# The first block's gates as a strand of their own, two heads' scores in one bank, norm factors applied behind the products, and a first mixer that does not yield to the second tile's block

## The chip, the cores and the metric

One core of a Trainium2 chip runs the whole program. The metric is the device time of one launch, in microseconds. The kernel before took 2147.11 us (median of three runs, 2147.04 to 2147.55).

## The reference

256 tokens of width 1024 pass one block of the first kind and two layers of the second kind, all in f32. Cut to what matters here:

```python
# first block (DEPTH = 1)
proj = rmsnorm(x, mix_norm_g) @ w_in            # 2560 columns of q/k/v, 3072 of gates
mkv  = rmsnorm(mem, mem_norm_g) @ w_mem_kv
gates = sigmoid(graw).reshape(B, S, 3, D_MODEL)
o_a = moba_attention(rope(rmsnorm(qa)), rope(rmsnorm(ka)), va) @ w_branch_moba     # 6 heads
o_d = dilated_attention(rope(rmsnorm(qd)), rope(rmsnorm(kd)), vd) @ w_branch_dil   # 6 heads
o_m = memory_attention(rmsnorm(qm), rmsnorm(mk), mv) @ w_branch_mem                # 4 heads
x = x + (gates[:,:,0]*o_a + gates[:,:,1]*o_d + gates[:,:,2]*o_m) @ w_out
u = causal_depthwise_conv(rmsnorm(x, ffn_norm_g) @ w_ffn_up)                       # 5632 columns
x = x + (silu(u_gate) * u_val) @ w_ffn_down
# second block, twice (l = 0, 1)
proj = rms_norm(x, norm1_g[l]) @ w_in[l]        # attention, convolution, RG-LRU
x = x + concat(forgetting_attention, conformer_conv, rglru_block) @ w_out[l]
xn = rms_norm(x, norm2_g[l])                    # peer: 8 heads route each token to 16 experts
x = x + sum_k gate_k * gelu(xn . u_tab[e_k]) * v_tab[e_k]      # 128 experts for each token
```

The expert tables are `peer`, one row of 8 KB (a row of u beside a row of v) for each expert. A token needs 128 rows in a layer.

## The kernel before

**Tiles and stages.** The tokens are two tiles, t = 0 and 1, of 128 on the partitions. B0 and B1 are the first block for the tiles, M00, M01, M10, M11 the mixers for layer l and tile t (M00 is layer 0, tile 0). A mixer ends with the routing, four times two heads, each of which writes 32 columns of `eidx` (L1802). Then come 128 gathers for this layer and tile: gather k brings the rows of expert k of all 128 tokens, 1 MB, by an indirect DMA of GpSimd (L2082). For each gathered MB VectorE makes a dot product with xn (`dot`, L1931), ScalarE a weight (`weigh`), and either TensorE adds the scaled row into PSUM (`down`, L1070) or VectorE adds it into x (L1941). There are 512 gathers, and none of a tile can start before its routing.

**Weights.** They are streamed as slabs of 2 MB (1.5 or 1 MB for some) into `ring`, three places of 16 KB a partition, by SyncE's queue (`slab`, L2098), in the order in which TensorE takes them (`take`); a slab is loaded once the slab three places before it (two, from the first gather on) is used up. A block takes 5 slabs of q/k/v, for B0 one of the memory, 6 of gates, 3 branches, 2 of w_out, 11 up and 6 down; a mixer takes 11. A token tile (L723) is 8 matmuls of 512 columns for each slab, a feature tile (L737) 32 of 128 columns. The trace has two records for each such f32 matmul, so a slab is 16 or 64 records.

**Places for gathered rows.** There are eight of 1 MB: 0 to 3 are `arena`, free when M00's key scores are done (`key_scores`); 4 and 5 are `kv1`, which holds the keys and values of the first block until the attention of B1 is over (`att_over`); 6 and 7 are the third place of `ring`.

**Order.** Each engine has a strand for each stage, written as a generator that yields after each step. A planner inside the program (`make_plan`) runs the strands against costs written by hand and writes a fixed order for TensorE, VectorE and ScalarE. Among the steps that are ready it takes the least `wish`, which is 1 plus 0.01 for each place in `STAGES`, so an earlier stage first. One rule speaks of M00: while TensorE has made fewer than `T_HEAD` = 80 steps of B1, M00 (with its strands R00 and C00) has the wish 1.3 and comes after B1. Engines run their fixed order; one that waits holds up all that stands behind it.

**B0.** Its gates run in `gate_chunks`, woven step by step with the heads by `weave` on all three engines. The norm of a tile is a chain (`rms_tile`): ScalarE squares, VectorE inverts, ScalarE takes the root, VectorE refines (`newton`) and multiplies x into scr (`scaled`, L1578); TensorE transposes that, then multiplies. The memory has the same chain (`mem_scaled`, L1590).

**Attention** goes by units of two heads: `scores` (L768), the row maximum on VectorE (L1469, or L1473 without a mask), the exponential on ScalarE, for the dilated heads counts on VectorE (L1484), transposes (L784), a copy, and `values` (L798). The scores of a unit have two PSUM banks, one for each head. Room.S, T and O are the banks for scores, transposes and outputs: B0 has two pairs for scores and one bank each for T and O; M00 and B1 have one of each.

## Time and profile before

| | |
|---|---|
| median of 3 runs | 2147.11 us |
| the profiled execution | 2146.26 us |
| its span | 2144.5 us |
| PE, DVE, ACT, POOL busy | 81%, 63%, 38%, 28% |
| DMA moved | 774.29 MB, mean 361 GB/s |
| granted clock of TensorE, mean | 0.92 |
| first gather | 534.5 us |

The page divides the span into 40 slices of 53.6 us. Its line DMA gives the mean busy share of the 16 DMA engines in tenths, and is read beside the line of PE: at each place one of the two is near 9. A timeline row gives the start and the length of a run of like instructions, the line of the kernel, and in brackets the idle time of that engine before it with what ended it.

### The profile page before, as it was taken

The page shows a single profiled execution, that of the slowest core. Times are in us where ns is not written, and L with a number is a line of the kernel's source. Part 1 is how long each engine was busy: PE and PEld are TensorE (multiplying, and loading weights), DVE is VectorE, ACT ScalarE, POOL GpSimd, SP SyncE. Part 2 cuts the span into 40 slices and gives each one's busy share as a digit, 9 for nine tenths or more (in the row PEclk, how much of TensorE's full clock was granted, in tenths as well). Part 3 has the DMA queues.
Part 4 walks back from the last instruction along what each step waited for, and adds up shares of the span by engine and source line. Part 5 has one row for each costly group of instructions (what it writes and reads, how often), then busy time and mean ns, then how long its engine had stood idle before and what let it go on. Part 6 is the DMA issues. An engine that isn't in the chain of part 4 may idle for free.

```text
span 2144.5 us, 21045 instructions
## 1 busy us (share of the span) xinstructions
PE 1746.1 (81%) x6904; PEld 1012.3 (47%) x6904; DVE 1348.5 (63%) x3432; ACT 807.3 (38%) x2104; POOL 595.3 (28%) x516
## 2 busy tenths in 40 slices
PE   7988989889878888977767877767798777677776
PEld 3447847547567464453324633623364362222222
DVE  2423314713988558757886786588888658885444
ACT  2232201520456436523434354134437414333333
POOL 0000000000222223533444353234443324434331
PEclk9989999799989999989989898978999988879999
DMA  9556767157999999999999999999999998999997
GB/s 359 214 199 235 290 241 293 50 229 263 385 417 406 418 414 407 416 420 406 410 409 418 411 412 402 419 361 419 420 419 420 419 378 321 394 383 415 420 420 311
DMA packets 108526, 774.29 MB, mean 361 GB/s; under 512 B 12160, under 2 KB 12416, under 8 KB 16256
## 3 DMA queue, kind: packets, MB, share of 16 engines
q0 software_dynamic: 73728, 536.90, 61.2%
q1 hardware_dynamic: 34688, 236.04, 27.8%
q8 instruction: 54, 0.88, 0.2%
q14 instruction: 56, 0.46, 0.1%
HBM read 771.85 MB, written 1.05 MB: 360 GB/s over the span
## 4 chain that ended last, share of the span: by engine, by line
PE 40%; DMA 34%; DVE 14%; issue 5%; ACT 4%; POOL 3%; SPq 0%; DVEq 0%; POOLq 0%; ACTq 0%
DMA kv<-in_peer_dram,eidx 12%; PE psum L1070 10%; DMA arena<-in_peer_dram,eidx 10%; PE psum L723 8%; PE psum L737 8%; DMA ring<-in_slabs_dram 7%; PE psum L927 5%; DMA ring<-in_peer_dram,eidx 4%; PE psum L945 3%; POOL arena L2082 1%; DVE arena L1931 1%; PE psum L902 1%; DVE kv L1931 1%; DVE x L1941 1%; DMA wf<-in_wf_dram 1%
## 5 line engine op out<-in xcount | busy, mean ns | idle before, releaser
L1070 PE MATMUL psum<-arena,diag 128*128 128x512 f32 x824 | 425.5, 651 | 127.9 <-ACT diag L1393 124.8
L2082 POOL DMA_INDIRECT arena<-in_peer_dram,eidx x258 | 306.3, 1187 | 479.3 <-PE psum L1070 367.6
L1931 DVE CUSTOM_DVE_ANT_0 arena<-arena,osb 128x1024 f32<-128x1024 f32 x258 | 314.0, 1223 | 163.4 <-DMA arena<-in_peer_dram,eidx 162.7
L2082 POOL DMA_INDIRECT kv<-in_peer_dram,eidx x130 | 147.8, 1137 | 828.5 <-DVE eidx L1802 534.0
L1383 ACT ACTIVATE wexp<-hid 128x1 f32<-128x1 f32 x512 | 103.0, 201 | 702.4 <-DVE hid L1931 701.6
L1070 PEld LDWEIGHTS psum<-arena,diag 128*128 128x128 f32 x824 | 159.2, 206 | 355.0 <-ACT diag L1393 198.8
L1070 PE MATMUL psum<-kv,diag 128*128 128x512 f32 x428 | 219.0, 640 | 60.7 <-ACT diag L1393 56.7
L723 PE MATMUL psum<-ring,hT 128*128 128x512 f32 x560 | 252.0, 603 | 4.4 <-DMA ring<-in_slabs_dram 1.6
L1070 PE MATMUL psum<-ring,diag 128*128 128x512 f32 x376 | 197.0, 654 | 71.5 <-ACT diag L1393 71.3
L1931 DVE CUSTOM_DVE_ANT_0 kv<-kv,osb 128x1024 f32<-128x1024 f32 x130 | 158.6, 1222 | 82.4 <-DMA kv<-in_peer_dram,eidx 81.9
L737 PEld LDWEIGHTS psum<-hT,ring 128*128 128x128 f32 x1536 | 184.3, 199 | 34.6 <-DMA ring<-in_slabs_dram 18.1
L2082 POOL DMA_INDIRECT ring<-in_peer_dram,eidx x124 | 141.0, 1137 | 213.2 <-PE psum L1070 176.4
L737 PE MATMUL psum<-hT,ring 128*128 128x128 f32 x1536 | 185.4, 283 | 17.4 <-DMA ring<-in_slabs_dram 15.2
L1931 DVE CUSTOM_DVE_ANT_0 ring<-ring,osb 128x1024 f32<-128x1024 f32 x124 | 151.0, 1223 | 59.1 <-DMA ring<-in_peer_dram,eidx 58.6
L927 PE MATMUL psum<-hT,ring 128*128 128x130 f32 x1408 | 169.2, 283 | 18.4 <-DMA ring<-in_slabs_dram 9.2
L927 PEld LDWEIGHTS psum<-hT,ring 128*128 128x128 f32 x1408 | 167.9, 198 | 28.3 <-issue 15.6
L723 PEld LDWEIGHTS psum<-ring,hT 128*128 128x128 f32 x560 | 106.8, 194 | 133.0 <-issue 126.9
L1393 ACT ACTIVATE diag<-const,wexp 128x128 f32<-128x128 f32 x407 | 163.4, 401 | 13.4
L1070 PEld LDWEIGHTS psum<-kv,diag 128*128 128x128 f32 x428 | 81.9, 203 | 171.8 <-ACT diag L1393 89.8
L1070 PEld LDWEIGHTS psum<-ring,diag 128*128 128x128 f32 x376 | 73.8, 207 | 178.1 <-ACT diag L1393 105.1
L1386 ACT ACTIVATE wexp<-wexp,sm 128x1 f32<-128x1 f32 x512 | 150.8, 294 | 16.6
L945 PE MATMUL psum<-ring,scr 128*128 128x512 f32 x176 | 80.1, 614 | 11.7 <-DMA ring<-in_slabs_dram 11.7
(315 smaller groups left out, 1794.1 us busy)
## 6 DMA issues: line engine op xcount, KB each, us to landing
ring<-in_slabs_dram SPq DMA_DIRECT2D x206, 1024.0 KB, 6.9
ring<-in_slabs_dram SPq DMA_DIRECT2D x8, 768.0 KB, 5.5
arena<-in_peer_dram,eidx POOLq DMA_INDIRECT x258
ring<-in_slabs_dram SPq DMA_DIRECT2D x8, 512.0 KB, 4.3
kv<-in_peer_dram,eidx POOLq DMA_INDIRECT x130
kk<-in_keys_dram SPq DMA_DIRECT2D x2, 1024.0 KB, 11.0
ring<-in_peer_dram,eidx POOLq DMA_INDIRECT x124
rowg<-in_rows_dram SPq DMA_DIRECT2D x3, 512.0 KB
```

Of the source, the lines that this page charges most:

```text
L723: ins = pe.matmul(bank(b), hT_[:, k, :], wk[:, k, :], start=(k == 0), stop=(k == 7))
L737: ins = pe.matmul(bank(b)[:, 128 * i:128 * i + 128], wk[:, k, 128 * i:128 * i + 128], hT_[:, k, :], start=(k == 0), stop=(k == 7))
L902: ins = pe.matmul(bank(b), oT[:, k0 + k, :], wk[:, k, 512 * h:512 * h + 512], start=(k == 0), stop=(k == kb - 1))
L927: ins = pe.matmul(bank(b)[:, 256 * gv:256 * gv + 130], wk[:, k, cw:cw + 128], hTe[:, k, :], start=(k == 0), stop=(k == 7))
L945: ins = pe.matmul(bank(b), act[:, f, :], wk[:, k, 512 * h:512 * h + 512], start=(f == 0), stop=(f == 21))
L1070: ins = pe.matmul(bank(b), diags_of(n), pair(slot_of[n])[:, 1024 + 512 * h:1536 + 512 * h], start=(k == 0), stop=(k == 127))
L1383: act.activation(wn, hid[:, 128 * t + k:128 * t + k + 1], ACT.Gelu_apprx_tanh).then_inc(*up("gelu", n))
L1386: act.activation(wn, wn, ACT.Copy, scale=gate[t][:, k:k + 1]).then_inc(*up("weight", n))
L1393: act.activation(diags_of(n), ident, ACT.Copy, scale=wn).then_inc(*up("diag", n))
L1931: v.tensor_tensor_reduce(out=row, in0=row, in1=row_y[t], scale=1.0, scalar=0.0, op0=ALU.mult, op1=ALU.add, accum_out=hid[:, c:c + 1]).then ...
L1941: v.scalar_tensor_tensor(x3[:, t, :], pair(slot_of.get(n, 0))[:, 1024:2048], wexp[:, c:c + 1], x3[:, t, :], ALU.mult, ALU.add).then_inc(*u ...
L2082: pool.indirect_dma_start(pair(i), None, tables, bass.IndirectOffsetOnAxis(ap=eidx[:, 128 * t + k:128 * t + k + 1], axis=0)).then_inc(sig. ...
```

## The change

1. **T_HEAD is 0**, so M00 never has the wish 1.3 and stands before B1 at every choice.
2. **Gates as a strand.** B0's six gate slabs become a stage G0 of their own, with a place in `STAGES` right behind B0; its loads stand in the order in which it takes them. The first branch of B0 waits for the last gate.
3. **Two heads' scores in one bank.** `scores` writes both heads into one bank, and the second head's matmul waits until the first has ended (`pe_step`). The banks that come free give B0 a second one for T and for O, M00 and B1 a second one for scores, and the later mixers a second one for T.
4. **Norms behind the products.** For the first norm of B0 and B1 and for the memory, the raw x is transposed and multiplied, and the factor is applied as `scale` of the ScalarE copy or sigmoid that empties the bank. The two kinds of scaling on VectorE (`scaled` "h", `mem_scaled`) are gone; the norm before the FFN and those of the mixers stay.

```diff
-T_MB, T_SEEN, T_ISSUE, T_DOT, T_WEIGHT, T_DIAG, T_TENSOR, T_VECTOR, T_TABLE, T_HOP, T_KEEP, T_LEAN, T_AHEAD, T_LATE, T_PACE, T_SHRINK, T_FLIGHT, T_END, T_HEAD = 2.5, 2.0, 1.15, 1.35, 0.55, 0.42, 2.0, 1.35, 1.28, 0.12, 4, -2.0, 14, 0.0, 3.0, 0, 8, 0, 80
+T_MB, T_SEEN, T_ISSUE, T_DOT, T_WEIGHT, T_DIAG, T_TENSOR, T_VECTOR, T_TABLE, T_HOP, T_KEEP, T_LEAN, T_AHEAD, T_LATE, T_PACE, T_SHRINK, T_FLIGHT, T_END, T_HEAD = 2.5, 2.0, 1.15, 1.35, 0.55, 0.42, 2.0, 1.35, 1.28, 0.12, 4, -2.0, 14, 0.0, 3.0, 0, 8, 0, 0
...
-            "B0": Room(range(8), (0, 6), (2,), (4,), scr, hT, tmp),
-            "M00": Room((0, 1, 2, 3, 0, 1, 2, 3), (0,), (2,), (3,), arena[:, 0:2816], arena[:, 3072:5120], arena[:, 5120:8192]),
-            "B1": Room((4, 5, 6, 7, 4, 5, 6, 7), (4,), (6,), (7,), scr, hT, tmp),
+            "B0": Room(range(8), (0, 1), (2, 6), (4, 7), scr, hT, tmp),
+            "M00": Room((0, 1, 2, 3, 0, 1, 2, 3), (0, 1), (2,), (3,), arena[:, 0:2816], arena[:, 3072:5120], arena[:, 5120:8192]),
+            "B1": Room((4, 5, 6, 7, 4, 5, 6, 7), (4, 5), (6,), (7,), scr, hT, tmp),
         }
         for m in ("M01", "M10", "M11"):
-            room[m] = Room((4, 5, 1, 3, 4, 5, 6, 7), (4, 6), (1,), (3,), scr, hT, tmp)
+            room[m] = Room((4, 5, 1, 3, 4, 5, 6, 7), (4, 6), (1, 5), (3,), scr, hT, tmp)
...
-        STAGES = ("B0", "M00", "R00", "C00", "B1", "Q00", "M01", "R01", "C01", "Q01", "M10", "R10", "C10", "Q10",
+        STAGES = ("B0", "G0", "M00", "R00", "C00", "B1", "Q00", "M01", "R01", "C01", "Q01", "M10", "R10", "C10", "Q10",
...
@@ -760,16 +764,19 @@
 
                 def scores(i):
                     u, n = units[i], r.S[i % len(r.S)]
-                    s3 = psum[:, 512 * n:512 * n + 1024].rearrange("p (h k) -> p h k", h=2)[:, :, 0:u.nk]
+                    s3 = bank(n).rearrange("p (h k) -> p h k", h=2)[:, :, 0:u.nk]
                     for done in ready:
                         w.wait_ge(*done)
+                    wait_bank(n)
                     for h in range(2):
-                        wait_bank(n + h)
                         ins = pe.matmul(s3[:, h, :], u.q(h), u.k(h), start=True, stop=u.bias is None)
                         if u.bias is not None:
                             ins = pe.matmul(s3[:, h, :], *u.bias(h), start=False, stop=True)
+                        if h == 0:
+                            ins.then_inc(*own.up())
+                            w.wait_ge(*own.now())
                     ins.then_inc(*up("att_scores", s, i))
-                    bank_free[n] = bank_free[n + 1] = at("att_top", s, i, 1) if u.mask is not None else at("att_exp", s, i, 1)
+                    bank_free[n] = at("att_top", s, i, 1) if u.mask is not None else at("att_exp", s, i, 1)
...
-                yield from turn_tile(s, scr_[:, 0:1024], b_[6:8], "turned_v", at("scaled", s, "h"), "h")
+                yield from turn_tile(s, x3[:, t, :], b_[6:8], "turned_v", (sig.sem("l_x%d" % t), 16), "h")
...
-                if t == 0:
-                    yield from weave(heads(), gate_chunks())
-                else:
-                    yield from heads()
+                yield from heads()
...
+                    if t == 0:
+                        w.wait_ge(*at("gates_out", t, 5))
...
+            def first_gates():
+
+                b_, hTt = room["B0"].bank, hT_tile("B0")
+                w.wait_ge(*at("turned_v", "B0", "h", 1))
+                for c in range(6):
+                    after = at("gates_out", 0, c - 2) if c > 1 else at("mem_out", 1, 1) if c else at("turned_v", "B0", "h", 1)
+                    yield from token_tile("G0", (b_[5], b_[3])[c % 2], hTt, "gates", 0, c, after=after)
...
                     w.wait_ge(*at("qkv", t, c))
+                    w.wait_ge(*at("rms", s))
                     for i, (d, of) in enumerate(pieces(s, t, c)):
-                        act.activation(d, bank(b_[c % 2])[:, of], ACT.Copy).then_inc(*up("qkv_out", t, c, i))
+                        act.activation(d, bank(b_[c % 2])[:, of], ACT.Copy, scale=sm[:, 641 + 3 * t:642 + 3 * t]).then_inc(*up("qkv_out", t, c, i))
...
-                y = yield from rms_tile(s, "h")
-                w.wait_ge(*own.now())
-                v.tensor_scalar(xs, x3[:, t, :], y, None, ALU.mult).then_inc(*up("scaled", s, "h"))
+                yield from rms_tile(s, "h", "rms", s)
...
-                        for u in range(2):
-                            v.tensor_scalar(mem_s[:, u, :], mem3[:, u, :], ym[:, u:u + 1], None, ALU.mult).then_inc(*up("mem_scaled", u))
```

**TensorE around M00's key scores, before.** `kk` are the keys; L737 with `arena` is M00's query projection, L723 with `hT` a gate or w_out slab of B1, L902 a branch of B1:

```order
L723 MATMUL psum<-ring,arena 128x512 x16
L723 MATMUL psum<-ring,hT 128x512 x6
L751 MATMUL psum<-const,osb 128x128 x8
L737 MATMUL psum<-arena,ring 128x128 x128
L902 MATMUL psum<-ring,scr 128x512 x3
L1036 MATMUL psum<-kk,arena 128x128 x16
L902 MATMUL psum<-ring,scr 128x512 x3
L723 MATMUL psum<-ring,hT 128x512 x16
```

**After**, the same place (line numbers are 4 to 8 higher: L741 is the old L737, L1044 the old L1036, L873 the old L872, the transposes of B1's queries and keys; L772, L791, L805 the attention):

```order
L755 MATMUL psum<-const,osb 128x128 x8
L727 MATMUL psum<-ring,hT 128x512 x6
L741 MATMUL psum<-arena,ring 128x128 x64
L727 MATMUL psum<-ring,hT 128x512 x2
L741 MATMUL psum<-arena,ring 128x128 x64
L873 MATMUL psum<-const,scr 128x128 x4
L1044 MATMUL psum<-kk,arena 128x128 x16
L873 MATMUL psum<-const,scr 128x128 x10
L772 MATMUL psum<-kv,scr 128x256 x4
```

Before, B1's whole attention, four of its gate slabs, one branch and half of the next stand ahead of the key scores. After, only B1's five q/k/v slabs and four transposes stand there; its attention stands behind.

**SyncE behind B0's last slab, before.** A slab of 2 MB is two loads of 128x2048; 128x1536 is a branch of B1:

```order
L2098 DMA ring<-in_slabs_dram 128x2048 x24
L2098 DMA ring<-in_slabs_dram 128x1536 x2
L2098 DMA ring<-in_slabs_dram 128x2048 x16
L2098 DMA ring<-in_slabs_dram 128x1536 x2
L2098 DMA ring<-in_slabs_dram 128x2048 x4
L2098 DMA ring<-in_slabs_dram 128x1024 x2
```

**After:**

```order
L2095 DMA ring<-in_slabs_dram 128x2048 x36
L2095 DMA ring<-in_slabs_dram 128x1536 x2
L2095 DMA ring<-in_slabs_dram 128x2048 x4
L2095 DMA ring<-in_slabs_dram 128x1536 x2
L2095 DMA ring<-in_slabs_dram 128x2048 x4
L2095 DMA ring<-in_slabs_dram 128x1024 x2
```

Eighteen slabs stand ahead of B1's first branch instead of twelve: the 11 of M00, 5 of q/k/v and 2 of gates.

**GpSimd's first gathers with their waits, before:**

```order
L2082 DMA kv<-in_peer_dram,eidx 128x2048 [waits routed,att_over]
L2082 DMA kv<-in_peer_dram,eidx 128x2048
L2082 DMA arena<-in_peer_dram,eidx 128x2048 [waits qp,key_scores]
L2082 DMA arena<-in_peer_dram,eidx 128x2048 x3
L2082 DMA ring<-in_peer_dram,eidx 128x2048 [waits branch]
L2082 DMA ring<-in_peer_dram,eidx 128x2048
L2082 DMA kv<-in_peer_dram,eidx 128x2048 [waits row4,down_mm]
```

**After:**

```order
L2079 DMA arena<-in_peer_dram,eidx 128x2048 [waits routed,qp,key_scores]
L2079 DMA arena<-in_peer_dram,eidx 128x2048 x3
L2079 DMA arena<-in_peer_dram,eidx 128x2048 [waits down_mm]
L2079 DMA kv<-in_peer_dram,eidx 128x2048 [waits att_over]
L2079 DMA kv<-in_peer_dram,eidx 128x2048
L2079 DMA ring<-in_peer_dram,eidx 128x2048 [waits gates]
L2079 DMA ring<-in_peer_dram,eidx 128x2048 [waits row0]
```

The first four go into `arena`; the fifth waits for a `down` and the sixth and seventh for `att_over`, which stands behind B1's attention.

Counted in VectorE's order: 49 dots stand ahead of B1's last add into x before, 57 after; ahead of M01's first write of `eidx` 121 and 124.

## Rows read from the trace of the kernel before

**Rows 1.** The page, part 2: the DMA engines in 40 slices.

```profile
DMA  9556767157999999999999999999999998999997
```

**Rows 2.** Windows: stretch, its length, busy of each engine, PEclk, DMA share, GB/s.

```profile
268.00:536.00 268.00, 245.46 (x1130) 159.56 (x1128) 101.91 (x355) 62.99 (x133) 1.24 (x2) 0.93 0.57 215
...
375.00:417.00 42.00, 33.64 (x173) 23.80 (x172) 33.81 (x144) 25.37 (x72) 0.00 (x0) 0.79 0.17 66
...
516.00:536.00 20.00, 20.00 (x52) 8.97 (x50) 17.67 (x68) 2.71 (x4) 1.24 (x2) 1.00 0.60 211
...
590.00:1000.00 410.00, 344.41 (x1650) 228.73 (x1649) 286.52 (x678) 192.23 (x455) 126.63 (x107) 0.93 1.00 414
```

**Rows 3.** Timeline of PE, 300 to 517: start, length, instruction, records, idle before.

```profile
305.54 35.16 PE L723 MATMUL psum<-ring,hT 128*128 128x512 f32 x80
...
340.53 14.45 PE L737 MATMUL psum<-arena,ring 128*128 128x128 f32 x128
...
371.78 1.10 PE L872 MATMUL psum<-const,scr 128*128 128x128 f32 x8 [0.76 <-DVEq L1652]
...
412.78 3.53 PE L798 MATMUL psum<-kv,tmp 128*128 128x64 f32 x16
...
452.56 13.90 PE L723 MATMUL psum<-ring,arena 128*128 128x512 f32 x32
...
472.02 1.09 PE L751 MATMUL psum<-const,osb 128*128 128x128 f32 x8 [0.42 <-DVE osb L1913]
...
512.84 3.73 PE L1036 MATMUL psum<-kk,arena 128*128 128x128 f32 x32
```

**Rows 4.** Timeline of VectorE, 348 to 534.

```profile
348.63 0.55 DVE L1620 TENSOR_TENSOR tmp<-scr 128x384 f32<-128x384 f32 x1
...
466.49 0.69 DVE L1567 TENSOR_TENSOR x<-x,psum 128x512 f32<-128x512 f32 x1 [6.18 <-PE psum L723]
...
516.68 0.50 DVE L1740 MAX8 sm<-psum 128x8 f32<-128x128 f32 x2 [2.22 <-PE psum L1036]
...
533.35 0.19 DVE L1802 TENSOR_TENSOR eidx<-junk 128x32 uint32<-128x32 f32 x1
```

**Rows 5.** Waits of GpSimd: who waited for whom, total, times, longest.

```profile
POOL kv L2082 <- DVE eidx L1802: 534.0, 1, 534.0
```

**Rows 6.** The page, part 6: the slab loads.

```profile
ring<-in_slabs_dram SPq DMA_DIRECT2D x206, 1024.0 KB, 6.9
...
ring<-in_slabs_dram SPq DMA_DIRECT2D x8, 768.0 KB, 5.5
...
ring<-in_slabs_dram SPq DMA_DIRECT2D x8, 512.0 KB, 4.3
```

**Rows 7.** Groups of VectorE by form, 371 to 417: busy, mean ns, idle before.

```profile
L1469 DVE CUSTOM_DVE_ANT_0 tmp<-psum,const 128x256 f32<-128x256 f32 x12 | 4.7, 422 | 0.3 <-DVE keep L1895 0.2
...
L1484 DVE CUSTOM_DVE_ANT_0 tmp<-tmp,const 128x256 f32<-128x256 f32 x6 | 2.3, 420 | 0.0
```

**Rows 8.** Timeline of PE in the first block.

```profile
12.52 36.65 PE L723 MATMUL psum<-ring,hT 128*128 128x512 f32 x80 [1.57 <-DMA ring<-in_slabs_dram]
...
66.34 25.91 PE L723 MATMUL psum<-ring,hT 128*128 128x512 f32 x60
...
101.78 0.49 PE L768 MATMUL psum<-kv,scr 64*128 64x128 f32 x4 [0.69 <-ACT kv L1226]
...
132.65 1.97 PE L751 MATMUL psum<-const,scr 128*128 128x128 f32 x8 [0.59 <-DVE scr L1501]
```

**Rows 9.** Timeline of VectorE in the first block.

```profile
75.58 0.20 DVE L1425 TENSOR_TENSOR sm<-sm 128x36 f32<-128x36 f32 x1 [6.06 <-ACT sm L1106]
```

**Rows 10.** Timeline of VectorE: end of B1, and the routing of M01.

```profile
768.27 1.28 DVE L1567 TENSOR_TENSOR x<-x,psum 128x512 f32<-128x512 f32 x2 [20.53 <-PE psum L945]
...
1003.53 0.19 DVE L1802 TENSOR_TENSOR eidx<-junk 128x32 uint32<-128x32 f32 x1
```

**Rows 11.** Timeline of GpSimd: the first gather that needs that routing.

```profile
1008.13 0.94 POOL L2082 DMA_INDIRECT ring<-in_peer_dram,eidx  x1 [0.31 <-PE psum L1070]
```

More of the change, by code:

```diff
@@ L1268, in block, with first_gates @@
                 for _ in range(22):
+                    yield
+            def first_gates():
+                b_ = room["B0"].bank
+                for c in range(6):
+                    w.wait_ge(*at("gates", 0, c))
+                    w.wait_ge(*at("rms", "B0"))
+                    act.activation(gates[:, c // 2, 512 * (c % 2):512 * (c % 2) + 512], bank((b_[5], b_[3])[c % 2]), ACT.Sigmoid,
+                                   scale=sm[:, 641:642]).then_inc(*up("gates_out", 0, c))
                     yield
@@ L2132, in block @@
                     yield
-                    for c in range(6):
-                        slab(S_GATE + c)
-                        yield
                     for br in range(3):
@@ L2156, in block, with first_gates @@
                     yield
+            def first_gates():
+                for c in range(6):
+                    slab(S_GATE + c)
+                    yield
             def mixer(l, t):
```

76 lines of the change are left out of this document (30 added, 46 removed).

## The prediction

> **What bounds the kernel now.** I read the page's slices first. From the eleventh on the DMA engines are at nine tenths nearly everywhere, before it they are at 5 to 7 and once at 1 [rows 1]. Then the windows: 0.57 from 268 to 536, 1.00 with 414 GB/s from 590 to 1000 [rows 2]. So the kernel has two halves with different limits. From about 536 on it moves bytes at full rate, and only fewer bytes or an earlier start can shorten it. Until then TensorE sets the pace, and what the DMA engines leave unused there is lost. The turning point is the first gather: GpSimd waited 534.0 us once for the routing (`eidx`) and never again [rows 5]. The timeline shows what stood before it: B1's q/k/v, M00's first slabs, then from 371.8 to 416.3 B1's transposes and attention [rows 3], with the DMA engines at 0.17 [rows 2], then gates of B1 and M00's rest mixed, the key scores at 512.8 [rows 3] and 16.7 us of routing [rows 4].
>
> The time is therefore: when the DMA engines become full, plus the bytes then left over 0.413 MB per us (I take 413 of the 414 GB/s). An edit that moves the start must be charged for the bytes that it pushes behind it.
>
> **T_HEAD: the first gather.** I rebuild M00 on the clock of before, with B0's end unchanged. A slab costs TensorE 35.16/5 = 7.0 us as a token tile and 14.45/2 = 7.2 as a feature tile [rows 3].
> - M00's norm no longer stands behind B1's scaling, so its first slab starts about 1 us before B1's did (305.5), at 304.5. Two feature slabs, the forget gates, two more, the small gates, v: 14.4 + 1.9 + 14.4 + 1 + 7.0, to 343.
> - Then attention of M00 (8 us of TensorE work with the small products) with 30 of the 40 q/k/v matmuls of B1 between, 30 x 0.88 = 26.4, to 379. VectorE was busy 33.8 of 42 us with M00's and B1's work together [rows 2]; with M00's alone I take it to be no later than TensorE.
> - w_out 13.9, to 393; its norm as before, from w_out's end at 466.3 to the transposes at 472.0 with B1's matmuls inside [rows 3], 5.7, to 398.5; the transposes 1.1; six matmuls of B1 5.3; four feature slabs with two matmuls between 28.8 + 1.8, to 435.5.
> - The order puts four transposes of B1 ahead of the key scores, and these wait for B1's head norms. Before, these ran from 348.6 to 371.8 with 3.5 us of other work, so 19.5 [rows 3, 4]; they can start when the last q/k/v slab is out at 421, with a root 1.5 later: 442.5. Key scores 3.7, to 447. This is a new wait of 7 us, and it is in the sum.
> - Routing 533.5 - 516.7 = 16.8, less the 1.4 of a branch of B1 in it, plus two of B1's row maxima at 0.9: about 17, first gather at 465 instead of 534.5, 70 us earlier.
>
> **But the start of the full stretch is later than that.** Only four places are free at 465. They fill in 4 x 1.05/0.413 = 10 us. The slabs gate 0, gate 1 and the first branch were loaded since 436 and no place of the ring falls free, since B1's attention runs without weights. Places 4 and 5 wait for its end. Behind the key scores VectorE has two routings of 15.4, two dots of 1.2 and that attention: 4.7 + 2.3 [rows 7] + about 6 for the maxima of the memory heads, the negations, accumulator reads and outputs, 13; in all 46, so attention ends at about 493. VectorE sets this pace, so the second bank for scores is worth 0 to 3 us here, and I take 0. So full from 493 instead of 536: 43 us earlier.
>
> **The bytes behind it.** By 536 the kernel had loaded 14 full slabs of B1 (5 q/k/v, 6 gates, 2 w_out, one up) and 3 branches: 14 x 2.097 + 2 x 1.573 + 1.049 = 33.55 MB. By 493 it will have 7 full slabs, one branch and 5 gathers: 14.68 + 1.57 + 5.24 = 21.5 MB (sizes in [rows 6]). 12.05 MB more remain, at 0.413: 29 us. The net is -43 + 29 = -14. The idle stretch of 375 to 417 does not go away, it moves to about 475 to 493 and is shorter, as gathers lie in it.
>
> [...]
>
> **B0.** The gates no longer hold the heads. VectorE waited 6.06 us for the root of the head norms [rows 9], which stood on ScalarE behind a gate's sigmoid; in the new order it stands ahead, so the heads are normed 3 to 4 us earlier. When the first scores come, 38 of 48 gate matmuls are done before and 28 after, 10 x 25.91/30 = 8.6 us less ahead of the scores [rows 8]; the same matmuls now fill the attention, which took 132.65 - 101.78 = 30.9 us. If they fit into its gaps B0 gains 8.6, if none does, 0. I take the middle and a little more: -5. Raw x into the transposes gives nothing in B0, as the first product waited for the first slab [rows 8]; what it gives in B1 is in the 304.5. The factors as `scale` ride on copies that exist.
>
> The wait between two heads: 8 units in B0, 8 in B1, 16 in the mixers. A pair of score matmuls takes 0.49 us in all [rows 8], so a wait costs between 0 and about that. In B0 8 x 0.2 = 1.6 is in the 5; elsewhere other strands lie beside. [...]
>
> **The hand-over to the second tile.** In the full stretch the next tile's routing must come before gathers run out. Before, B1 ended at 768.3, M01's first `eidx` came at 1003.5, 235 us later [rows 10], and the first gather that needs it went at 1008.1 [rows 11]. The new order has 57 dots ahead of B1's end instead of 49. B1's end by bytes: 493 + ((768 - 536) x 0.413 + 12.05 + 8 x 1.05)/0.413 = 774, less B0's 5, 769. The 71 gathers then left and M01's 11 slabs are 74.5 + 23.1 = 97.6 MB, 236 us, so they last to 1005; with 235 us the routing comes at 1004 and the DMA engines run dry for the time of a gather, some 4 us: +4. Later tiles have the same counts of dots as before.
>
> **Sum.** -43 + 29 - 5 + 4 = -15. Against the profiled execution's own 2146.26 this is 2131; its medians lie 0.85 higher: **2132**.
>
> **Rivals.**
> - *More overlap* (the gap at 475 to 493 is shorter and the gates fit into B0's attention): attention 8 us earlier, B0 9 instead of 5, no hand-over loss: -15 - 8 - 4 - 4 = -31, 2116. For it: M00 and B1 have second banks. Against: VectorE is what counts there.
> - *The new stretch is not full.* From 493 B1 does gates, branches and w_out, with two ring places instead of three. If the DMA share is 0.87 instead of 1.00 for the first 110 us, 14 us go and the result is 2146, no change. For it: with gates alone the share was 0.60 from 516 to 536 [rows 2]. Against: no gathers were there then.
> - *Slower: the strand of the second tile.* TensorE was at 344 of 410 us [rows 2], and about 70 us of B1's gates and w_out now lie in the full stretch. If B1 and M01 fall behind their gathers, gather 129 has no index and the DMA engines stand idle, one us for each. It costs from 1 us past the forecast; at 15 us it eats the gain (a strand of 250 instead of 235), and at a tenth more, 258, it is -15 + 23 = +8, 2155.
> - *The order does not carry over:* M00 comes only half as early on the chip since the fixed order stalls on other waits; -43 becomes -35, about 2140.
>
> **Chances.** Forecast 0.45, more overlap 0.17, order half carried over 0.08, not full 0.13, slower 0.17. The forecast's own range is 2122 to 2142. For 8 in 10 I reach to 2110 and 2155. What can be told from no change is about 0.2%, 4.3 us. Faster by more: 0.45 + 0.17 + 0.08 = 0.70; same 0.13; slower 0.17.
>
> **What would show it.** First `eidx` between 452 and 466 (465 less B0's 5 is 460). A DMA share near 0.2 for some 15 us before GpSimd's sixth gather, which should go between 480 and 495. The transposes behind B0's attention at 124 to 130 instead of 132.65. B1's last add into x near 769 with 57 dots done. A GpSimd wait for `eidx` near 1000: under 6 us for the forecast, over 20 for the slower rival. A first gather after 485, or a share below 0.9 from 500 to 600, would make it wrong.

## The result, and the profile after

The changed kernel takes **2171.8 us** (median of four runs, 2164.8 to 2179.0) against 2147.1 for the kernel before in the same comparison: ratio 1.0129, 95% interval 1.0107 to 1.0150. It is slower by some 25 us where 15 us faster was forecast. The profiled execution took 2173.97 us with a span of 2172.2, against 2144.5 before; the explanation below is of these 27.7 us.

What was meant to happen first did happen. The rows below are of TensorE's timeline (PE) in the kernel after, then of GpSimd's (POOL): start, length, instruction, number of records, idle time before and what ended it.

```profile
128.25 1.09 PE L755 MATMUL psum<-const,scr 128*128 128x128 f32 x8 [0.58 <-DVE scr L1510]
...
297.67 17.30 PE L741 MATMUL psum<-arena,ring 128*128 128x128 f32 x128 [0.78 <-DVE arena L1460]
...
373.85 13.90 PE L727 MATMUL psum<-ring,arena 128*128 128x512 f32 x32
...
446.04 3.81 PE L1044 MATMUL psum<-kk,arena 128*128 128x128 f32 x32 [0.34 <-ACT arena L1335]
...
464.43 1.12 PE L791 MATMUL psum<-const,tmp 128*128 128x128 f32 x4 [9.96 <-ACT tmp L1149]
...
476.17 2.49 PE L772 MATMUL psum<-kv,scr 64*128 64x256 f32 x4
...
483.06 2.49 PE L772 MATMUL psum<-kv,scr 64*128 64x256 f32 x4
...
501.69 3.51 PE L1078 MATMUL psum<-arena,diag 128*128 128x512 f32 x4
```

The transposes behind B0's attention begin at 128.25 instead of 132.65 [rows 8], w_out of M00 begins at 373.85 instead of 452.56 and the key scores at 446.04 instead of 512.84 [rows 3]. Behind them stands B1's attention, a pair of heads every 6.9 us (476.17, 483.06), and nearly at its end, at 501.69, the first addition of a gathered row (a "down", L1078: two matmuls, four records). GpSimd shows what that means:

```profile
467.86 1.07 POOL L2079 DMA_INDIRECT arena<-in_peer_dram,eidx  x1 [467.41 <-DVE eidx L1799]
...
471.72 0.94 POOL L2079 DMA_INDIRECT arena<-in_peer_dram,eidx  x1 [0.31 <-issue]
505.48 1.51 POOL L2079 DMA_INDIRECT arena<-in_peer_dram,eidx  x1 [32.82 <-PE psum L1078]
508.82 0.93 POOL L2079 DMA_INDIRECT kv<-in_peer_dram,eidx  x1 [1.83 <-DVEq L1659]
...
530.95 1.83 POOL L2079 DMA_INDIRECT arena<-in_peer_dram,eidx  x1 [11.55 <-PE psum L1078]
554.36 1.00 POOL L2079 DMA_INDIRECT arena<-in_peer_dram,eidx  x1 [21.58 <-PE psum L1078]
```

The first gather goes 66.6 us earlier than before (467.9 for 534.5). The fifth waits 32.82 us for the first down, the kv places open at 508.8, and then two more waits, 11.55 and 21.58 us, are for the second and third down, which stand in TensorE's fixed order behind gates and branches of B1. The gathers flow only from about 555.

Windows, kernel before (stretch, length, busy of each engine, PEclk, DMA share, GB/s):

```profile
0.00:430.00 430.00, 386.94 (x1814) 254.78 (x1815) 162.45 (x537) 113.12 (x262) 0.20 (x4) 0.93 0.61 235
430.00:555.00 125.00, 116.20 (x519) 73.10 (x517) 47.87 (x167) 24.49 (x42) 7.96 (x8) 0.97 0.70 273
555.00:800.00 245.00, 207.52 (x1107) 149.14 (x1105) 169.54 (x431) 120.46 (x261) 61.66 (x54) 0.93 0.99 407
800.00:1100.00 300.00, 237.76 (x874) 130.81 (x872) 230.69 (x589) 132.81 (x354) 122.56 (x102) 0.94 1.00 413
1100.00:1500.00 400.00, 303.20 (x1104) 168.50 (x1104) 296.96 (x704) 160.72 (x449) 157.55 (x131) 0.88 0.99 405
```

The same windows, kernel after:

```profile
0.00:430.00 430.00, 387.29 (x1857) 255.94 (x1858) 146.92 (x484) 110.14 (x235) 0.20 (x4) 0.96 0.64 248
430.00:555.00 125.00, 103.43 (x406) 65.56 (x406) 96.19 (x358) 42.01 (x90) 11.93 (x11) 0.78 0.54 205
555.00:800.00 245.00, 199.78 (x955) 135.41 (x955) 144.93 (x271) 120.95 (x240) 66.64 (x55) 0.90 1.00 412
800.00:1100.00 300.00, 237.24 (x969) 141.62 (x968) 226.79 (x549) 122.13 (x322) 102.44 (x88) 0.88 0.96 390
1100.00:1500.00 400.00, 311.06 (x1100) 168.62 (x1099) 292.77 (x727) 160.03 (x439) 145.44 (x127) 0.88 0.97 396
```

Read these as a ledger: length times GB/s is what was moved (GB/s is rounded, so each sum is good to about 0.3 MB). By 430 the changed kernel is 5.6 MB ahead (106.6 against 101.1). By 555 it is 2.9 behind (25.6 MB in 125 us against 34.1), by 800 still 1.7, by 1100 8.6, by 1500 12.2. A lead at the start became a debt within the very stretch that was to pay, and 300 us in which nothing of the change seems to lie added 6.9 MB, 17 us.

The milestones of the second tile, VectorE's timeline after, answer to [rows 10]:

```profile
795.13 1.29 DVE L1576 TENSOR_TENSOR x<-x,psum 128x512 f32<-128x512 f32 x2 [23.20 <-PE psum L945]
...
1030.40 0.19 DVE L1799 TENSOR_TENSOR eidx<-junk 128x32 uint32<-128x32 f32 x1
```

B1 ends at 795.1 instead of 768.3, and M01 is routed at 1030.4 instead of 1003.5, 235.3 us later as before. From that routing to the end of the span it is 1141.8 us, before 1141.0. So, counted by milestones, the whole loss is there when M01 is routed. Counted by bytes it is not: by 1100 the debt is worth 21 us and by 1500 it is worth 30, so some 9 us (3.6 MB) of it arise well behind that routing.

Where the flow is thin behind 800 can be read from two windows and from GpSimd, kernel after:

```profile
920.00:940.00 20.00, 20.00 (x46) 8.73 (x45) 13.24 (x18) 4.84 (x18) 8.54 (x8) 0.97 0.67 255
1020.00:1040.00 20.00, 16.63 (x38) 6.70 (x36) 17.17 (x49) 9.27 (x25) 10.90 (x10) 0.99 0.89 342
```

```profile
924.69 1.24 POOL L2079 DMA_INDIRECT kv<-in_peer_dram,eidx  x1 [9.21 <-PE psum L1078]
...
1021.03 0.93 POOL L2079 DMA_INDIRECT arena<-in_peer_dram,eidx  x1 [12.87 <-PE psum L1078]
...
1031.37 1.27 POOL L2079 DMA_INDIRECT arena<-in_peer_dram,eidx  x1 [2.15 <-DVE eidx L1799]
```

Against 413 GB/s the first window lacks 3.2 MB and the second 1.4. Both lie behind waits of GpSimd for a down, 9.21 and 12.87 us. For M01's routing itself GpSimd waits only 2.15 us.

### The profile page after: what moved, and what is told of

Its sections match the earlier page's. It is cut to its first block, busy times and chain, and to the rows that moved or that the text cites. A ratio compares the mean times of both kernels' runs of the same rounds, so it can differ in the third digit from the quotient of the medians.

```text
span 2172.2 us, 20901 instructions
## 1 busy us (share of the span) xinstructions
PE 1758.4 (81%) x6824; PEld 1014.5 (47%) x6824; DVE 1373.8 (63%) x3448; ACT 823.8 (38%) x2099; POOL 585.9 (27%) x516
## 4 chain that ended last, share of the span: by engine, by line
PE 45%; DMA 36%; DVE 10%; ACT 3%; issue 3%; POOL 2%; SPq 0%; POOLq 0%; ACTq 0%; DVEq 0%
DMA ring<-in_slabs_dram 11%; PE psum L1078 11%; PE psum L727 10%; DMA arena<-in_peer_dram,eidx 9%; DMA kv<-in_peer_dram,eidx 8%; PE psum L741 8%; DMA ring<-in_peer_dram,eidx 8%; PE psum L927 6%; PE psum L945 3%; PE psum L772 2%; DVE x L1938 1%; PE psum L902 1%; PE psum L805 1%; DVE arena L1928 1%; DVE kv L1928 1%
## 5 line engine op out<-in xcount | busy, mean ns | idle before, releaser
L2079 POOL DMA_INDIRECT arena<-in_peer_dram,eidx x258 | 295.6, 1146 | 976.1 <-DVE eidx L1799 469.6
L1078 PE MATMUL psum<-arena,diag 128*128 128x512 f32 x764 | 397.7, 654 | 117.2 <-ACT diag L1402 106.4
L1078 PEld LDWEIGHTS psum<-arena,diag 128*128 128x128 f32 x764 | 149.3, 207 | 331.5 <-ACT diag L1402 176.0
L1078 PE MATMUL psum<-kv,diag 128*128 128x512 f32 x416 | 220.3, 657 | 82.8 <-ACT diag L1402 82.7
L727 PE MATMUL psum<-ring,hT 128*128 128x512 f32 x560 | 262.9, 622 | 13.6 <-DMA ring<-in_slabs_dram 8.5
L1078 PE MATMUL psum<-ring,diag 128*128 128x512 f32 x368 | 197.6, 665 | 58.5 <-ACT diag L1402 58.2
L2079 POOL DMA_INDIRECT ring<-in_peer_dram,eidx x124 | 139.6, 1126 | 259.6 <-PE psum L1078 171.5
L741 PEld LDWEIGHTS psum<-hT,ring 128*128 128x128 f32 x1536 | 182.9, 198 | 35.4 <-DMA ring<-in_slabs_dram 16.1
L741 PE MATMUL psum<-hT,ring 128*128 128x128 f32 x1536 | 184.6, 282 | 17.1 <-DMA ring<-in_slabs_dram 12.6
L1078 PEld LDWEIGHTS psum<-kv,diag 128*128 128x128 f32 x416 | 80.7, 206 | 200.0 <-ACT diag L1402 117.4
L1402 ACT ACTIVATE diag<-const,wexp 128x128 f32<-128x128 f32 x387 | 155.4, 401 | 12.6
L1078 PEld LDWEIGHTS psum<-ring,diag 128*128 128x128 f32 x368 | 71.7, 209 | 164.2 <-ACT diag L1402 97.3
```

What stands on the lines that cost most here:

```text
L727: ins = pe.matmul(bank(b), hT_[:, k, :], wk[:, k, :], start=(k == 0), stop=(k == 7))
L741: ins = pe.matmul(bank(b)[:, 128 * i:128 * i + 128], wk[:, k, 128 * i:128 * i + 128], hT_[:, k, :], start=(k == 0), stop=(k == 7))
L1078: ins = pe.matmul(bank(b), diags_of(n), pair(slot_of[n])[:, 1024 + 512 * h:1536 + 512 * h], start=(k == 0), stop=(k == 127))
L1402: act.activation(diags_of(n), ident, ACT.Copy, scale=wn).then_inc(*up("diag", n))
L2079: pool.indirect_dma_start(pair(i), None, tables, bass.IndirectOffsetOnAxis(ap=eidx[:, 128 * t + k:128 * t + k + 1], axis=0)).then_inc(sig. ...
```

## The experiments

Spans and rows are those of the profiled execution; times are medians of the timed runs, and ratios are to the kernel before in the same comparison.

**Which part costs: e1 and e2.** Apart from T_HEAD the two kernels of the comparison differ in the gates' strand, the one-bank scores and the late norms.

```
e1: the changed kernel  -T_HEAD 0   +T_HEAD 80
e2: the kernel before   -T_HEAD 80  +T_HEAD 0
```

> The changed kernel with T_HEAD put back to 80: the gates as a strand, the pair of scores in one bank with its wait, the norms behind the products, and the old order of M00 against B1. Theory (the yielding of the order is what costs): the loss is gone, first gather at 527 to 534 us, B0 some 5 to 8 us earlier, 2137 to 2144 us, ratio 0.995 to 0.999. Rival (the wait inside a score pair slows all attention, and the order is innocent): the slow attention stays, 2155 us or more.

> The kernel before with T_HEAD 0 and nothing else. Theory: the order alone costs what was lost and what the other parts save besides, about +30 us: 2170 to 2182 us, first gather at 470 to 475 and a hole after the fourth gather. Rival (the pair wait does it): with scores in two banks and no wait B1's attention is short, the hole is under 15 us, and the time is at or below 2147.

e1: 2149.0 us, ratio 1.0028 (1.0015 to 1.0042). e2: 2171.5 us, ratio 1.0142 (1.0119 to 1.0166), first gather at 454.7 and the fifth at 494.6 after a wait of 35.16. T_HEAD alone carries the loss; scores in two banks without a wait do not close the hole. The other parts together aren't the gain that theory said (2137 to 2144, first gather at 527 to 534; it came at 539.6), but a loss of some 4 to 6 us, no more than p1 to p3 below find for a mere shuffle of the order. The timeline of TensorE in e1 shows one cost among them:

```profile
297.45 36.70 PE L727 MATMUL psum<-ring,hT 128*128 128x512 f32 x80 [4.61 <-DVE hT L1460]
333.99 1.04 PE L755 MATMUL psum<-const,arena 128*128 128x128 f32 x8
355.17 3.35 PE L873 MATMUL psum<-const,scr 128*128 128x128 f32 x14 [20.14 <-DVEq L1651]
```

q/k/v of B1 begin 8.1 us before those of [rows 3]. But M00's transposes now stand behind them, so its feature slabs no longer fill the time of B1's head norms, and TensorE waits 20.14 us.

**Other places for M00: e3, e4, e6, e7.** T_HEAD 60 and 50 let M00 go ahead for a part of B1's steps; the other two give M00 a condition.

```
e3: T_HEAD 60      e4: T_HEAD 50
e6 (T_HEAD 80):
-  if s in ("M00", "R00", "C00") and at_step["PE", "B1"] < T_HEAD:
+  if s in (...) and at_step["PE", "B1"] < T_HEAD and at_step["PE", "M00"] >= 24:
e7 (T_HEAD 80):
+  if s in (...) and at_step["PE", "B1"] < T_HEAD and not (
+      at_step["PE", "B1"] > 30 and at_step["PE", "M00"] < 24):
```

> The changed kernel with T_HEAD 60 instead of 0: B1's q/k/v and most of its attention stand beside M00's first slabs, and four units of that attention no longer stand behind the key scores. Theory (what hurts at 0 is that B1's attention comes after the first gathers with only four places open and downs behind it): the first gather comes at 480 to 505, the places in kv are open by then, full flow from about 515 to 535, time 2125 to 2145. Rival (any order that lets M00 ahead delays B1's end and with it every later tile): B1's last add into x after 780 and a time of 2155 or more.

> The changed kernel with T_HEAD 50: as with 60, but M00's slabs start earlier and more of B1's attention is spread over them and w_out; none of it stands behind the key scores. Theory: first gather at 470 to 495, kv places open within 10 us of it, time 2125 to 2150. Rival as with 60: B1's end after 780 and 2155 or more.

> The changed kernel with T_HEAD 80, and M00 yields only from its small gates on: four feature slabs of M00 first, then B1's q/k/v, then both attentions mixed, M00's output product, two gates of B1, the key scores. B1's attention ends ahead of the first gather, as in the kernel before. Theory (a first gather helps where places are open and B1's strand isn't held): first gather at 490 to 515, full flow within 15 us of it, B1's last add into x at 755 to 770, 2120 to 2138 us. Rival (the mixed attentions run at a low clock with TensorE waiting, as with T_HEAD 50 and 60): first gather at 515 or later, 2150 or more.

> As the run before, but M00 yields to B1's q/k/v first: q/k/v, M00's four feature slabs and small gates, then both attentions mixed. Theory: the hole of 20.1 us is gone, first gather at 505 to 525, B1's last add at 758 to 768, 2125 to 2140 us. Rival: the mixed attentions cost what the hole cost, 2143 to 2155.

All four are slower: 2188.6 us (1.0216), 2189.0 (1.0217), 2179.2 (1.0188) and 2168.9 (1.0123). The first gathers came at 523, 516, 520 and 559, later than each theory said; e6's rival (515 or later, 2150 or more) was right. In e3 and e4 the wait of 20.1 us of e1 is there as well, and where the attentions are mixed the granted clock from 410 to 440 was 0.57, 0.62, 0.69 and 0.50. The rivals of e3 and e4 had the time, and e4's also B1's end (805.3; in e3 it came at 778.6, not behind 780); e7 is slower than both of its ranges. My theory of a good place for M00 fell in all four.

**The hole of e1, and the pair's wait: e5 and e9.** e5 lets M00's norm and transposes stand ahead of B1's q/k/v again; e9 is e5 with the scores in two banks.

```
e5 (T_HEAD 80):
+  if s in (...) and at_step["PE", "B1"] < T_HEAD and at_step["PE", "M00"] >= 6:
e9 = e5, and
-  s3 = bank(n)...               +  s3 = psum[:, 512 * n:512 * n + 1024]...
-  if h == 0: ins.then_inc(*own.up()); w.wait_ge(*own.now())
   and the rooms of the kernel before
```

> The changed kernel with T_HEAD 80, and M00 yields only from its first slab on: its norm and eight transposes stand ahead of B1's q/k/v again, so its four feature slabs can fill the time in which B1's heads are normed. The trace of the kernel with T_HEAD 80 alone has TensorE idle for 20.1 us there, and the kernel before has none. Theory (the three other parts save 6 to 7 us in B0, and this hole ate them): the hole is under 2 us, the first gather comes at 520 to 527 instead of 539, and the time is 2130 to 2139 us. Rival (the pair wait or something later eats the saving): first gather at 534 or later and 2143 to 2150.

> The kernel of e5 (T_HEAD 80, M00 yields from its first slab on) with the scores of a pair of heads in two banks and without the wait between them, as in the kernel before; the other parts stay. Theory (the wait in a pair keeps TensorE at its lower clock through B1's attention and lengthens it): from the end of M00's second pair of slabs to the end of B1's attention 45 us as before instead of 53, the granted clock there 0.75 or more instead of 0.60, first gather at 530 to 534 instead of 541. The order behind B1's end changes with it, so the total is less sure: 2138 to 2150. Rival (the clock falls there for another reason): 52 to 54 us and a clock near 0.60 again.

e5: the hole is gone, and the first gather still comes at 540.7; 2153.9 us, ratio 1.0038 (1.0023 to 1.0054). The rival had the first gather (534 or later); its time, 2143 to 2150, was passed by 4 us. e9: first gather at 529.8, 2149.2 us, ratio 1.0028 (1.0011 to 1.0045). TensorE's timeline, e5:

```profile
370.01 1.09 PE L873 MATMUL psum<-const,scr 128*128 128x128 f32 x8 [0.76 <-DVEq L1651]
...
406.15 2.49 PE L772 MATMUL psum<-kv,scr 64*128 64x256 f32 x4
...
412.96 2.49 PE L772 MATMUL psum<-kv,scr 64*128 64x256 f32 x4
423.08 1.97 PE L755 MATMUL psum<-const,scr 128*128 128x128 f32 x8 [0.59 <-DVE scr L1510]
```

and e9:

```profile
364.76 1.10 PE L870 MATMUL psum<-const,scr 128*128 128x128 f32 x8 [0.75 <-DVEq L1648]
...
393.06 1.23 PE L772 MATMUL psum<-kv,scr 64*128 64x256 f32 x4
...
398.69 1.23 PE L772 MATMUL psum<-kv,scr 64*128 64x256 f32 x4
...
413.09 1.97 PE L755 MATMUL psum<-const,scr 128*128 128x128 f32 x8 [0.59 <-DVE scr L1507]
```

A pair takes 2.49 us with the wait and 1.23 without, a unit 6.8 instead of 5.6, and the stretch from the first transposes to those behind the attention 53.1 us instead of 48.3 (45.1 in the kernel before). So the wait, with the bank rooms that go with it, costs about 5 us of the strand ahead of the first gather, which the forecast priced at nothing. (Another 5 us of the earlier first gather come from before: e9's transposes begin at 364.8 instead of 370.0, and not by the wait alone, since the changed kernel, with the wait, ends B0 as early as e9, at 288.3 and 287.3; e5 at 293.8.) My reason was half wrong: the clock did not rise with the wait gone. From 385 to 415 it was 0.60 in e5 and 0.50 in e9 (0.73 before). The wait is therefore not what holds the clock low; that it is the chain of a unit through three engines is my reading, and no run shows it by itself. e9 routes M01 at 989.6, 14 us before the kernel before, and does not end earlier in the timed runs.

**Is it an accident of the order? p1 to p3.** The planner's hop is changed by 0.01 us, which moves small things only.

```
p1: the kernel before, T_HOP 0.12 -> 0.13    p2: 0.12 -> 0.11
p3: the changed kernel, T_HOP 0.12 -> 0.13
```

> The kernel before with the planner's hop of 0.13 instead of 0.12 us: no work, wait or place changes; the order is the same up to B1's gated product and differs in small things behind it. Theory (the times hang on how well the fixed order of the full stretch fits the chip, and the order of the kernel before is one of the good ones): first gather and B1's end as before within 3 us, and yet 2150 to 2175 us, the loss in dips of the DMA share behind 800. Rival (an order as good as any other): within 4 us of before.

> As the run before with a hop of 0.11. Theory: 2150 to 2175 us, with first gather and B1's end unmoved. Rival: within 4 us of before.

> The changed kernel with the planner's hop of 0.13: the order is the same up to M00's first gathers. If the order of the full stretch decides (theory), the time lies anywhere from 2150 to 2200 while first gather and the hole behind the fourth stay at 466 to 470 and 30 to 35 us. If the change costs by its start alone (rival), it stays within 5 us of 2172.

Ratios 1.0003 (0.9986 to 1.0020), 1.0032 (1.0015 to 1.0048) and 1.0167 (1.0130 to 1.0204). Such changes are worth up to about 10 us (p3 against the changed kernel's own 1.0129), so the two or three tenths of a per cent of e1, e5 and e9 aren't to be read closely, but 25 us is no accident: the kernel before and its two neighbours lie at 1.0000 to 1.0032, the three orders with T_HEAD 0 (the changed kernel, p3, e2) at 1.0129 to 1.0167. The theory of p1, 2150 to 2175, fell; p2, at 2152.7, lies at its lower edge and outside its rival; p3 at 2182.3 lies outside its rival's 5 us. p3 is a help in another way. Windows of p3:

```profile
800.00:1000.00 200.00, 166.20 (x801) 108.49 (x800) 150.45 (x316) 88.41 (x224) 78.93 (x61) 0.93 1.01 416
1000.00:1100.00 100.00, 61.73 (x164) 28.76 (x162) 81.05 (x247) 31.72 (x95) 32.51 (x30) 0.83 0.86 345
```

and GpSimd in p3:

```profile
1010.33 0.94 POOL L2079 DMA_INDIRECT ring<-in_peer_dram,eidx  x1 [4.35 <-PE psum L1078]
1032.32 1.34 POOL L2079 DMA_INDIRECT ring<-in_peer_dram,eidx  x1 [21.05 <-PE psum L1078]
```

It moves at full rate until the 128th gather at 1010, and then GpSimd has nothing to issue for 21.05 us, since M01 is routed at 1031.4. The DMA engines still have gathers under way; from 1020 to 1040 they move 115 GB/s, so 6.0 MB or 14 us are missing. The sum from 800 to 1100, 83.2 + 34.5 = 117.7 MB, is nearly the changed kernel's 117.0. The loss behind 800 has the same size whether it shows as a thin rate or as one gap. In p3 the first tile's gathers are used up when M01's routing comes. The changed kernel also has issued all 128 by then, but it lost its time before, in waits for downs; that those waits come of the late routing is not shown.

**The priority of gathers: e8.**

```
the changed kernel, T_KEEP 4 -> 2
```

> The changed kernel (T_HEAD 0) with T_KEEP 2 instead of 4: the order is the same until B1's end, and behind it 107 instead of 124 dots stand ahead of M01's first eidx, so the second tile's strand comes earlier against the gathers. Theory (part of the loss is made at the hand-over: gathers taken early leave too few to cover B1's end to M01's routing, and the DMA share is 0.94 to 0.96 from 900 to 1100): M01's first eidx at 1010 to 1022 instead of 1030, the share from 900 to 1100 at 0.98 or more, and 2150 to 2163 us. Rival (the loss is made before B1's end alone, and the rate behind it is set by bytes): first eidx may move but the time stays within 4 us of 2172.

2219.3 us, ratio 1.0348. M01 is routed at 999.3, 31 us earlier, with 107 dots ahead of it instead of 124, and the share from 1000 to 1100 falls to 0.85. Both theories were wrong. B1's end is nearly where it was (793.1), so the strand from there to the routing took 206.1 us: 235 is not its own length, but its length with some 70 dots between its steps. The earlier routing was worth nothing here by itself, with the gathers ahead of it put off: the rest of the span was 75 us longer.

**The hole and B1's end, each alone: q1 to q4.**

```
q1: the changed kernel; q4: the kernel before; both
-  if n < len(gathers):
+  if n < len(gathers) and (n < 36 or at_step["PE", "B1"] == len(ways["PE"]["B1"])):
q2: the changed kernel, in way_of
+  if e == "PE" and n == "B1" and 46 <= i < 70:
+      return [("run", 2.0, None)] + ways[e][n][i]
q3: q2, and the limit of q1 at 38
```

> The changed kernel, whose planner takes no dot past the 36th until TensorE has done B1's last step: 44 dots instead of 57 stand ahead of B1's last add into x, nothing else is ruled. Theory T1 (B1's end is set by the bytes ahead of it, the routing of M01 follows 235 us later, and the rest 1142 us after that): B1's end 13 MB = about 30 us earlier by bytes, or at least at 770 to 780 where TensorE holds it; M01's routing at 1005 to 1015, total 2145 to 2160. Rival R1 (bytes alone count, the order of gathers and slabs is neutral): B1's end moves, but the total stays within 5 us of 2172.

> The changed kernel with a planner that counts each of TensorE's 24 steps of B1's attention 2.0 us longer, so the first down stands behind the fourth pair of scores of it instead of behind the last, and 63 dots instead of 57 ahead of B1's end. Work is the same. The wait of 32.8 us ahead of the fifth gather should fall to under 15. T1: the earlier gathers only push B1's slabs back; B1's end stays at 795 or goes later, 2168 to 2185. Rival R2 (the hole behind the fourth gather is what was lost): the bytes at 555 rise by 3 MB or more and the time falls by 7 us or more, to 2165 or less.

> Both edits on the changed kernel, with the limit at 38 (46 dots ahead of B1's end). T1: B1's end at 770 to 782, M01's routing 235 later, and the total 2145 to 2160, a little below the run with the limit alone. R1 or R2 alone: 2165 or more with one of the two, as said there.

> The kernel before with the same limit of 36 (44 dots instead of 49 ahead of B1's end). T1, if bytes hold B1's end there too: B1's end at 755 to 763, M01's routing 8 us earlier, and a total of 2136 to 2142. If TensorE holds it, B1's end stays at 768, gathers are only later, and the time is 2147 to 2155.

q1 2185.9 us (1.0185), q2 2180.0 (1.0155), q3 2196.0 (1.0232), q4 2156.9 (1.0076). T1 as I had it fell: in q1 B1's end did come 22 us earlier, at 773.1, and M01's routing 9 us later, at 1039.4, because the held dots were now missing as transfers (DMA share 0.75 from 700 to 800) and had to be made up before it. In q2 the wait of 32.82 became 15.88, and the next one grew to 27.99 us:

```profile
488.72 0.94 POOL L2081 DMA_INDIRECT arena<-in_peer_dram,eidx  x1 [15.88 <-PE psum L1080]
517.65 0.93 POOL L2081 DMA_INDIRECT arena<-in_peer_dram,eidx  x1 [27.99 <-PE psum L1080]
```

The downs inside B1's attention brought one gather forward and held B1 back; its last add came at 816.0, and GpSimd had no index for 21.05 us until M01 was routed. In q4 B1's end came 20 us earlier, at 748.1, the routing 11 us later, at 1014.5, and T1's 2136 to 2142 were missed: what q1 showed holds in the kernel before too. q3 has both edits and both costs (B1's end 787.5, routed 1056.7). So R2 is not borne out, and it isn't refuted as a price either: this edit moved the hole and did not close it.

**Is the strand on the path? d1 and d2.** 15 us of VectorE work in M01's strand, with the same result.

```
+  if s == "M01":
+      for _ in range(11):
+          v.scalar_tensor_tensor(xn, x3[:, t, :], y, rowg[:, :], ALU.mult, ALU.mult).then_inc(*own.up())
+          w.wait_ge(*own.now())
```

> The kernel before with M01's normalised rows computed 12 times instead of once, one after the other on VectorE (11 x about 1.35, some 15 us more in the second tile's strand, same result). Theory T3 (what is lost behind 800 in the changed kernel is lost because its second strand has no slack against the first tile's gathers: about 236 us of transfers for a strand of 235, where the kernel before has 79 gathers and 11 slabs, 256 us): the delay finds 20 us of slack here and costs 0 to 6 us, 2145 to 2153. Rival R3 (the strand is on the path in both, as B1's end to M01's routing is 235 us in both): it costs about 15 in both, 2158 to 2165 here.

> The same 11 repeated instructions in the changed kernel. T3: no slack is left, so about 15 us are lost: 2183 to 2192 us, and the bytes moved from 800 to 1100 fall by a further 3 to 6 MB. R3: 2183 to 2192 here as well, and the same loss in the kernel before. If both lose under 5 us, the strand isn't what holds the hand-over at all.

d1: 2167.7 us, ratio 1.0120 (1.0100 to 1.0140), some 24 us. d2: 2184.5 us, ratio 1.0198 (1.0179 to 1.0217), some 14 us over the changed kernel. T3 said that the kernel before has 20 us of slack here; it has none. The windows of d1 from 555:

```profile
555.00:800.00 245.00, 210.03 (x1125) 152.24 (x1125) 170.29 (x438) 129.45 (x268) 57.58 (x51) 0.92 0.98 401
800.00:1100.00 300.00, 217.92 (x803) 119.88 (x803) 232.46 (x537) 122.03 (x330) 113.28 (x94) 0.86 0.95 389
```

This is the changed kernel's picture (390 GB/s from 800 to 1100) made out of the kernel before, with its T_HEAD untouched: M01 is routed 23.0 us later (1026.5), and the span is 21.3 longer. It is the nearest thing to a price, but not a clean one. The 11 instructions took 14.1 us and the strand grew by 27.5 (262.8); the planner had also laid the order anew, with 125 dots instead of 121 ahead of the routing. And d2 does not repeat the price: M01 is routed 17.9 us later than in the changed kernel (1048.3), its span is only 8.0 longer. There the gathers did run out, and GpSimd waits for that routing:

```profile
1049.24 1.33 POOL L2083 DMA_INDIRECT ring<-in_peer_dram,eidx  x1 [31.17 <-DVE eidx L1799]
```

**What the runs say together.** The routing of M01 comes at the later of two times. One is the strand: B1's last add into x plus 235 us. The other is the bytes: about 319 MB (what the kernel before had moved at 1003.5), since 121 to 128 dots stand ahead of that routing in VectorE's order; from what is moved by 800 the rest goes at 0.413 MB per us. Both constants are those of the kernel before, and the rule was put up after the runs, so it is a reading, not a test.

| run | B1's end | MB by 800 | strand | bytes | routed | span | span less routed |
|---|---|---|---|---|---|---|---|
| before | 768.3 | 235.0 | 1003 | 1004 | 1003.5 | 2144.5 | 1141 |
| after | 795.1 | 233.1 | **1030** | 1009 | 1030.4 | 2172.2 | 1142 |
| e1 | 771.8 | 233.5 | 1007 | 1008 | 1009.3 | 2146.1 | 1137 |
| e2 | 808.1 | 229.7 | **1043** | 1017 | 1039.1 | 2165.2 | 1126 |
| e4 | 805.3 | 224.4 | **1040** | 1030 | 1043.5 | 2188.2 | 1145 |
| p3 | 791.2 | 233.4 | **1026** | 1008 | 1031.4 | 2179.0 | 1148 |
| q1 | 773.1 | 221.8 | 1008 | **1036** | 1039.4 | 2186.9 | 1147 |
| q2 | 816.0 | 230.5 | **1051** | 1015 | 1046.1 | 2180.7 | 1135 |
| q3 | 787.5 | 217.8 | 1023 | **1046** | 1056.7 | 2194.6 | 1138 |
| q4 | 748.1 | 232.2 | 983 | **1011** | 1014.5 | 2154.8 | 1140 |

e5, p1 and p2 fit as e1 does. In d1 and d2 the strand itself was made longer. e3, e6, e7, e8 and e9 have only 107 to 115 dots ahead of the routing and lie outside the rule; their rest is longer, 1147 to 1217 us. More gathers are left there, but 17 of them (e8) are some 43 us at full rate, and its rest is 75 longer. The rule misses by up to 11 us (q3), and e2's rest is 15 shorter, which I can't explain. Where B1's end is the later bound, 235 us is what these orders gave and not a floor (e8: 206), so the rule says when M01 was routed, and not why.

## Why the prediction was wrong

- **B0, -5: right, its parts only in sum.** The transposes behind its attention stand at 128.25, inside 124 to 130, 4.4 us earlier. The scores began 8.4 us earlier (93.36), where 8.6 was worked out, but the attention took 34.9 us instead of 30.9: a pair of scores with the wait takes 1.03 us instead of 0.49, not the 0.2 more that the sum had. B0's last add came at 288.3 instead of 295.4; in the kernels with the new parts it lay at 287.3 to 293.8, in those without at 294.4 to 295.4.
- **First gather, 460: late by 8, the mechanism right.** The order carried over: the key scores ended at 449.9 where 447 less 5 was worked out. M00's first pair of slabs took 17.30 us instead of 14.45, at a granted clock of 0.82 from 297 to 315 (before 1.00 from 340 to 355), and its last pair waited 7.46 us for a slab.
- **"Full from 493": this step failed, and it carries 26 of the 43 us between forecast and result.** It has three errors. I let attention end at 493 by summing VectorE's work; it ended at 508. One wait was 9.96, and from 476 on a unit took 6.9 us while VectorE was busy 15.5 us of 25 and TensorE, with its pairs at 2.49 us, 19.6 of 25, so by my reading the trip from engine to engine set the pace. I counted five gathers by 493 and did not ask where the first *down* stands in TensorE's order: at the end of B1's attention, so that the fifth went at 505.5. And with the kv places open I took the flow for full. The second down stands behind two gates and a branch (32 + 12 records, a matmul has two), the third behind two more gates and a branch. The rival "not full" had the right place; its reason was two ring places instead of three, and its share 0.87 for the first 110 us. The trace has 0.78 from 493 to 600.
- **The ledger of that step.** -43 + 29 - 5 claims a lead of 19 us, 7.8 MB, once the flow is full. By 555 there was a debt of 2.9 MB. The difference, 10.7 MB, is 26 us, and by so much B1's last add was late: 795.1 instead of 769. The 8 more dots ahead of it were in the forecast (8.4 MB; the windows have 231.2 against 222.0 MB moved by B1's end, 9.2 more).
- **Hand-over, +4: mis-sized, and it carries the other 17 us.** "235 us" held to the tenth (235.3). But behind B1's last add 8 gathers fewer are left, and the forecast let the rest of the span be 16 us shorter for it. It was 1377.1 us, before 1376.2: nothing was paid back. Why is shown only in part. The slower rival (2155, chance 0.17) let the gathers run out ahead of the routing, with a wait for `eidx` of over 20 us as its sign. p3, q2 and d2 show just that, with waits of 21.05, 21.05 and 31.17 us; the 20 us of thinnest flow at that place lack 6.0, 4.1 and 4.6 MB against 413 GB/s (115 GB/s from 1020 to 1040, 208 and 181 from 1040 to 1060), so the DMA engines lose 10 to 14 us, less than GpSimd waits. The changed kernel itself has only 2.15 us of such a wait, and so not the rival's sign: its flow is thin in waits for downs, at 920 and at 1020 above all, and some 9 us are lost behind 1100.
- **Even with B1's end at 769 the -15 is doubtful.** By the constants of the table, routed at 1004 and 1141 behind it, the span would be 2145, no change. But the rest of the runs with 120 or more dots ahead of the routing goes from 1126 (e2) to 1148, so this stays open. It wasn't tried, since no edit gave a full stretch from 493.
- **The wait between two heads, nothing outside B0: wrong.** It costs some 5 us of B1's attention, at a granted clock of 0.60 in e5 and 0.50 in e9 (385 to 415). A pair took 2.49 us with it and 1.23 in two banks without it. No run has both heads in one bank without the wait, so that one bank needs it is not shown.

Shown is that T_HEAD makes the loss (e1, e2). What stays open is the price of the hole by itself (q2 moved it and did not close it), what thins the flow behind 800, and why e9, which routes M01 14 us earlier, doesn't end earlier. No version that ran beats the kernel before.

## What to carry to other kernels

A first gather 66.6 us earlier was worth nothing here, where the consumer that frees its place was not early too (the fifth gather waited 32.82 us for the first down): follow the place, from the gather to the dot to the down, through the fixed order of every engine before calling a stretch full. Where work is taken early ahead of a strand that starts the next tile, keep a ledger of bytes at two or three milestones, and date that strand's end by the later of two bounds, its own length and the bytes ahead of it (in the table this missed by up to 11 us). A late start of the next tile went with a longer span in every run with 120 or more dots ahead of it; an early one bought by putting gathers off (e8, 31 us earlier, 2219.3 us) cost more than it gave. And a lead that is gained ahead of a hand-over counts only if the rest gets shorter by it.
